# Four of eleven pairs of gate tiles computed by seven products of half blocks, with six gate tiles ahead of the first up unit

## What is computed

```python
D_FF = 2816
FFN_CONV_WIDTH = 3

def causal_dwconv(x, w):
    k_width = w.shape[0]
    s = x.shape[1]
    xp = jnp.pad(x, ((0, 0), (k_width - 1, 0), (0, 0)))
    return sum(xp[:, j:j + s] * w[j] for j in range(k_width))

        h = rmsnorm(x, ln2[l])
        gate = causal_dwconv(h @ w_gate[l], ffn_conv[l])
        x = x + (jax.nn.silu(gate) * (h @ w_up[l])) @ w_down[l]
    return rmsnorm(x, ln_f)
```

## Time and profile before

| | us |
|---|---|
| median of 3 runs | 2668.59 |
| lowest, highest | 2666.81, 2672.78 |
| the profiled execution | 2666.36 |
| its span, first to last instruction | 2664.5 |

### The profile page before, as it was taken

One profiled execution on the slowest core, in us unless ns is written; L12 is line 12 of the kernel. 1 busy time (PEld: TensorE's weight loads), 2 busy tenths in 40 slices (PEclk: granted clock), 3 DMA queues, 4 the chain that ended last, 5 costly groups with the idle time before them and its releaser, 6 DMA issues.

```text
span 2664.5 us, 36444 instructions
## 1 busy us (share of the span) xinstructions
PE 2474.7 (93%) x14220; PEld 1524.5 (57%) x14220; DVE 1385.3 (52%) x2603; ACT 1022.0 (38%) x1944; POOL 504.5 (19%) x342
## 2 busy tenths in 40 slices
PE   6998887899999999797969999999899998999998
PEld 4874566433333333675744434443677887788887
DVE  3596545335444445586442333333766654673745
ACT  5225552234444443626523222222453343442423
POOL 0222102001111011233100000000324311453533
PEclk9999999899999999899989999999999998999999
DMA  7215714689999998420039999999122011132221
GB/s 279 68 48 222 285 64 180 245 326 380 386 388 385 388 387 347 145 79 17 33 134 394 421 421 421 421 421 403 55 92 80 17 32 48 56 111 92 99 95 64
DMA packets 85514, 567.98 MB, mean 213 GB/s; under 512 B 11640, under 2 KB 12024, under 8 KB 20320
## 3 DMA queue, kind: packets, MB, share of 16 engines
q1 hardware_dynamic: 79944, 550.27, 52.4%
q0 software_dynamic: 3616, 11.80, 2.0%
q10 hardware_dynamic: 1784, 3.58, 0.4%
HBM read 550.92 MB, written 14.68 MB: 212 GB/s over the span
## 4 chain that ended last, share of the span: by engine, by line
PE 44%; DVE 3%; DMA 2%; ACT 1%; POOL 1%; issue 1%; DVEq 0%; ACTq 0%; POOLq 0%
PE PS L1193 11%; PE PS L1322 3%; PE PS L1323 3%; PE PS L1324 3%; PE PS L1310 2%; PE PS L1308 2%; PE PS L1309 2%; PE PS L1267 2%; PE PS L1298 2%; PE PS L932 1%; PE PS L1555 1%; PE PS L1557 1%; PE PS L1556 1%; DMA RF<-in_w_down_dram 1%; PE PS L1440 1%
## 5 line engine op out<-in xcount | busy, mean ns | idle before, releaser
L3004 POOL TENSOR_TENSOR WHL<-RING,WHL 128x1024 fp32r<-128x1024 f32 (+1 forms) x84 | 203.4, 2422 | 822.4 <-ACT WHL L1590 818.3
L1590 ACT ACTIVATE WHL<-RING 128x1024 fp32r<-128x1024 f32 (+1 forms) x158 | 149.8, 961 | 238.2 <-PE PS L1324 134.1
L1193 PE MATMUL PS<-RING,RF 128*64 128x512 f32 x816 | 187.2, 602 | 1.0 <-issue 0.7
L1193 PE MATMUL PS<-WIDE,RF 128*64 128x512 f32 x792 | 182.0, 596 | 0.0
L2169 DVE TENSOR_TENSOR WHL<-RING,WHL 128x1024 fp32r<-128x1024 f32 (+1 forms) x74 | 97.8, 1323 | 129.1 <-ACT WHL L1590 124.7
L1883 ACT ACTIVATE RF<-PS,MODS,MSC 128x128 f32<-128x128 f32 x192 | 73.2, 445 | 180.1 <-PE PS L1267 128.8
L1308 PE MATMUL PS<-RR,WHL 128*128 128x512 f32 x336 | 136.6, 406 | 3.7 <-DVE RR L2700 1.8
L1310 PE MATMUL PS<-RR,WHL 128*128 128x512 f32 x336 | 133.6, 398 | 0.0
L1309 PE MATMUL PS<-RR,WHL 128*128 128x512 f32 x336 | 132.6, 395 | 0.0
L1193 PE MATMUL PS<-RF 128*64 128x512 f32 x544 | 127.5, 596 | 0.4 <-DMA RF<-in_w_down_dram 0.4
L1193 PE MATMUL PS<-X,RF 128*64 128x512 f32 x528 | 123.0, 597 | 0.4 <-DMA X<-in_w_down_dram 0.4
(11 more groups left out here) (446 smaller groups left out, 5752.1 us busy)
## 6 DMA issues: line engine op xcount, KB each, us to landing
RING<-in_w_gate_dram SPq DMA_DIRECT2D x63, 1024.0 KB, 8.8
WIDE<-in_w_down_dram SPq DMA_DIRECT2D x52, 1024.0 KB, 11.9
RING<-in_w_up_dram SPq DMA_DIRECT2D x46, 1024.0 KB, 8.6
RING<-in_ada_w_dram SPq DMA_DIRECT2D x44, 1024.0 KB, 6.5
AR<-in_w_up_dram SPq DMA_DIRECT2D x37, 1024.0 KB, 10.4
X<-in_w_gate_dram SPq DMA_DIRECT2D x36, 1024.0 KB, 8.8
RF<-in_w_down_dram SPq DMA_DIRECT2D x31, 1024.0 KB, 13.8
RING<-in_w_in_dram SPq DMA_DIRECT2D x30, 1024.0 KB, 5.0
```

Source lines behind the costliest of these rows:

```text
L1193: ins = e.matmul(a[r:r + 64, :], xs[:, j, 0:64], w[:, i, :], start=begin and i < 2, stop=end and i > 1)
L1590: e.activation(h, unsplit(st), ACT.Copy).then_inc(act, A(("hi", st["i"])))
L3004: e.tensor_tensor(lo, unsplit(st), h.bitcast(F32), ALU.subtract).then_inc(pool, G(("lo", st["i"])))
```

## The change

Gate pairs 3, 5, 7 and 9 (`GATE7`) are also made by the seven products, with their own sums, splitting and additions. Their convolution can't read PSUM, so it reads `Q`: ACT makes the last tap (`tap`), DVE adds the other two (`conv7`, four instructions with both inputs in SBUF), then ACT does both `silu`.

PE's order is now: six gate tiles, up 0, gate pair 3, up 1, gates 8 and 9, up 2, gate pair 5, up 3, down; up 4, gates 12 and 13, up 5, gate pair 7, up 6, gates 16 and 17, up 7, down; up 8, gate pair 9, up 9, gates 20 and 21, up 10, down. The unit after a down product has its sums made during that product. Where a unit follows a unit, its sums stand at products 1 and 6 of the unit before it. The convolution of a direct gate tile stands one step of PE later than before. Of a unit's seven low parts POOL now makes those of products 7 and 3 (before: of 2 and 4), DVE the other five. On DVE and POOL the low parts listed beside a direct gate tile now stand one step of PE earlier; those listed beside a product of a unit stand as before, and the low parts of the first down weights, where they are listed beside a product, one step later.

```diff
+GATE7 = (3, 5, 7, 9)
...
-    ends = {t1 // 2 - 1: part for part, (t0, t1) in enumerate(FFN)}
-    order = [("gate", 0), ("gate", 1)]
-    for u in range(FFN[-1][1] // 2):
-        if u + 1 < FFN[-1][1] // 2:
-            order += [("gate", 2 * u + 2), ("gate", 2 * u + 3)]
-        order += [("product", u, p) for p in SEVEN]
-        if u in ends:
-            order += [("down", ends[u], 0), ("down", ends[u], 1)]
+    order, gates = [], 0
+    for part, (t0, t1) in enumerate(FFN):
+        for u in range(t0 // 2, t1 // 2):
+            while gates < min(u + 3 - part, FFN[-1][1] // 2) and not (part and u == t0 // 2):
+                if gates in GATE7:
+                    order += [("product", ("gate", gates), p) for p in SEVEN]
+                else:
+                    order += [("gate", 2 * gates), ("gate", 2 * gates + 1)]
+                gates += 1
+            order += [("product", ("up", u), p) for p in SEVEN]
+        order += [("down", part, 0), ("down", part, 1)]
...
+            if k[1] and following is not None:
+                plan += [("sum", following, i) for i in (1, 2, 3, 4)]
...
+        if waiting and (what == "gate" or k[1] == SEVEN[0]):
+            f = waiting.pop(0)
+            plan += [("conv", f), ("silu", f)]
...
+            (kind, u), p = k
+            if near and p in (1, 6) and order[n + 7 - SEVEN.index(p)][0] == "product":
+                plan += [("sum", following, i) for i in ((1, 2) if p == 1 else (3, 4))]
+            rest = [("gu", u), ("gh", u), ("gl", u)] if kind == "up" else [("tap", u), ("conv7", u), ("silu", 2 * u), ("silu", 2 * u + 1)]
+            plan += {1: [("E", k[0])], 6: [("U2", k[0]), ("C11", k[0])], 7: [("UB", k[0]), ("C22", k[0])],
+                     4: [("UC", k[0]), *rest]}.get(p, [])
...
-                          single=mode == "u", low=mode == "u" and m in (1, 6) or mode == "f" and cc % 256 == 128)
+                          single=mode == "u", low=mode == "u" and m in (4, 5) or mode == "f" and cc % 256 == 128)
...
-            late = n >= len(ahead) - (len(steps) - ffn) and loads[st["load"]]["name"] != "w_down2"
+            used = n - (len(ahead) - len(steps))
+            late = used >= ffn and steps[used]["single"]
...
+                elif what == "tap":
+                    u, = k
+                    e.wait_ge(dve, V["UC", ("gate", u)])
+                    if u > 2:
+                        e.wait_ge(dve, V["gl", u - 3])
+                    for h in range(2):
+                        w = V_FC + 44 + 2 * u + h
+                        e.activation(GS[u % 3][:, 512 * h:512 * h + 512], Q[:, 512 * h:512 * h + 512], ACT.Copy, scale=VEC[:, w:w + 1]
+                                     ).then_inc(act, A(("tap", 2 * u + h)))
...
+                elif what == "conv7":
+                    u, = k
+                    for j in range(2):
+                        for h in range(2):
+                            f, o, b = 2 * u + h, GS[u % 3][:, 512 * h:512 * h + 512], Q[:, 512 * h:512 * h + 512]
+                            w = V_FC + 22 * j + f
+                            if j == 0:
+                                e.wait_ge(act, A["tap", f])
+                            else:
+                                e.wait_ge(dve, V["shift", f])
+                            e.scalar_tensor_tensor(o[:, 2 - j:512], b[:, 0:510 + j], VEC[:, w:w + 1], o[:, 2 - j:512], ALU.mult, ALU.add
+                                                   ).then_inc(dve, V(("gate" if j else "shift", f)))
```

More of the change, by code:

```diff
@@ L113, in ffn_order @@
     return order
 def ffn_plan():
-    plan = []
-    for what, *k in ffn_order():
+    plan, order, waiting = [], ffn_order(), []
+    for n, (what, *k) in enumerate(order):
+        following = next((it[1] for it in order[n + 1:] if it[0] == "product" and it[2] == SEVEN[0]), None)
+        near = any(it[0] == "product" and it[2] == SEVEN[0] for it in order[n + 1:n + 8])
         if what == "down":
             plan += [(what, *k)]
+            if k[1] and following is not None:
+                plan += [("sum", following, i) for i in (1, 2, 3, 4)]
@@ L123, in ffn_plan @@
             continue
         plan += [("w",), (what, *k)]
+        if waiting and (what == "gate" or k[1] == SEVEN[0]):
+            f = waiting.pop(0)
+            plan += [("conv", f), ("silu", f)]
         if what == "gate":
             f, = k
-            if f > 1:
-                u = f // 2 - 1
-                plan += [("sum", u, 1 + f % 2 * 2), ("sum", u, 2 + f % 2 * 2)]
-            if f % 2 or f == 2:
-                plan += [("conv", f - 1), ("silu", f - 1)]
-            if 0 < f < 4:
-                plan += [("operand", {1: 5, 2: 6, 3: 7}[f])]
-        else:
-            u, p = k
-            last = FFN[-1][1] // 2 - 1
-            plan += {1: [("conv", 2 * u + 3), ("E", u), ("silu", 2 * u + 3)] if u < last else [("E", u)],
-                     2: [("operand", 4)] if u == 0 else [],
-                     6: [("U2", u), ("C11", u)], 7: [("UB", u), ("C22", u)], 4: [("UC", u), ("gu", u), ("gh", u), ("gl", u)]}.get(p, [])
-            if u == last - 1 and p in (6, 5):
-                plan += [("sum", last, i) for i in ((1, 2) if p == 6 else (3, 4))]
+            waiting.append(f)
+            if order[n + 2 - f % 2][0] == "product":
+                plan += [("sum", following, 1 + f % 2 * 2), ("sum", following, 2 + f % 2 * 2)]
+            if 0 < f < 5:
+                plan += [("operand", {1: 5, 2: 6, 3: 7, 4: 4}[f])]
+        else:
+            (kind, u), p = k
[4 more added lines that the diff above has]
+                     4: [("UC", k[0]), *rest]}.get(p, [])
@@ L232, in weight_steps @@
         elif what == "product" and more[0] == SEVEN[0]:
[L233 removed]
+            add("w_up2" if k[0] == "up" else "w_gate2", (), 0, 8, 256 * k[1], 256, "u")
             loads[-1]["unit"] = k
@@ L3173, in gpsimd @@
                     e.wait_ge(weights_in[ld["slot"]], 16 * ld["n"])
-                    if u:
-                        low_done(next(st for st in of_unit[u - 1]["steps"] if st["sum"] == i))
+                    if u in earlier:
+                        low_done(next(st for st in of_unit[earlier[u]]["steps"] if st["sum"] == i))
                     if i in (2, 4):
```

16 lines of the change are left out of this document (9 added, 7 removed).

## The result

The changed kernel takes 2680.48 us, median of 6 runs (2677.29 to 2682.44), the kernel before 2668.53 (6 runs, 2665.96 to 2672.78). The ratio is 1.0040 with a 95% interval of 1.0028 to 1.0052: slower by 12.0 us. That is 0.4% and clear of the spread of the runs. Forecast were 2680.0 and "slower", so the total came out as forecast. Several of its terms did not, and the experiments are about those.

The account below looks back on a forecast made before the run. PE was taken to bound the kernel. Products -4.5, gaps -8.6, start +3.2, chains +18.5 and clock +2.8 gave +11.4 us on the median of 2668.59: forecast 2680.0, range 2658 to 2690.

Parts of the forecast that it names:

- PE sets the time, products -4.5: Last stage: PE is the limit; four gate pairs at 10.08 instead of 11.20 us each save 4.5 us.
- The four gaps, -8.6: PE's waits and slow steps at gate 3, up 0, gate 4 and unit 10: 8.6 us saved if all went.
- The start, +3.2: Six gate tiles and up 0: 1.6 us stays at gate 3, 1.6 more for a late low part in up 0.
- the walk from gate 1 to product 7: DVE and ACT followed through gates 1 to 4: low part ready at 2332.3, PE wants it at 2330.7, 1.6 us lost.
- The chains, +18.5: Four runs of three successive units: DVE, taking turns with POOL, falls behind PE; losses 5.5, 5.1, 5.1 and 2.8 us.
- The wait behind `conv7`: Product 3 of the up unit after a gate unit: its low part comes 2.6 us late in the second chain.
- The signs named beforehand: Steps unchanged; two waits a chain, some 2 and 2.6 us; gate units' `UC` 3 us or more late; none at unit 10.
- The clock, +2.8: PE falling to 1.2 GHz behind long waits: two falls taken, between none and six, 1.4 us for one.
- The price of `conv7`: Each of its four DVE instructions was taken at 0.65 us, with 0.75 as upper bound.
- The sum: All terms together: +11.4 us, 2677.8 against the profiled execution, 2680.0 against the median.
- B: Rival, chance 0.22: DVE late only for `tap` and `conv7`, PE loses 2.6 us four times; +0.5 us, 2669.
- A: Rival, chance 0.20: the chains keep up, only waits at the start stay; -11.5 to -9.9 us, 2657 to 2659.

## Why the prediction was right, and where only in sum

- **PE sets the time, products -4.5.** Right. The steps are 0.233 and 0.120 as in the earlier trace rows, and the stage adds up to 0.1 us with them. The Trainium skill (TensorE: Matmul & The Clock Gate, section Back-to-back issue gap) would have four pairs cost 7 us more instead, by the prediction's estimate from its 81 and 131 ns, with 256 columns a third of the way up (the prediction says halfway). The traces disagree, with 120 and 233 ns, and the versions with and without gate units, both nearly free of waits, bear them out: 1.9 less.
- **The four gaps, -8.6.** Those at gate 4 and unit 10 went and that at gate 3 stayed, as foreseen. That at product 6 of up 0 should have gone, and 1.56 of it stayed. And 8.6 was the size in one execution; the second has 13.5 (9.7 in waits and 3.8 in slow steps). This base was taken for fixed.
- **The start, +3.2.** 5.4 in waits, with a clock fall 7.2. (There is also a slip in the prediction: 2307.96 + 3 x 5.6 + 4 x 1.44 is 2330.5 and not 2330.7, so its own numbers give 1.8 for 1.6.) The step that failed is the walk from gate 1 to product 7: it ends the convolution of gate 4 at 2329.8 and gives no loss at product 6. With the 3.8 by which the stage starts earlier in this trace added, that convolution ended at 2332.1 (2328.3), 2.3 later than walked, and the two high parts behind its `silu` began at once (2328.35 and 2328.89 in the rows above). That `silu` ahead of the high part is the cause is shown by the run that moved it, in which both waits go.
- **The chains, +18.5.** 13.6 measured. The wait behind `conv7` was sized well (2.6 against 2.75, 2.75, 2.73, 2.37), that behind `gh` not (2.1 against 0.77, 0.77, 1.41 and none). The timelines of DVE and ACT in the second chain, whose walk the prediction gives:

```profile
2385.31 0.68 DVE L3000 TENSOR_TENSOR CON<-PS,CON 128x512 f32<-128x512 f32 x1
2386.09 1.81 DVE L3017 TENSOR_TENSOR AR<-CON,AR 128x1024 f32<-128x1024 f32 x1
...
2397.59 0.68 DVE L3000 TENSOR_TENSOR CON<-PS,CON 128x512 f32<-128x512 f32 x1
2399.06 2.74 DVE L3011 SCALAR_TENSOR_TENSOR AR<-CON,VEC,AR 128x510 f32<-128x510 f32 x4 [0.79 <-ACT AR L2166]
```

```profile
2387.94 1.06 ACT L2175 ACTIVATE AS<-AR 128x1024 fp32r<-128x1024 f32 x1 [5.07 <-DVE AR L3017]
2388.91 0.61 ACT L1601 ACTIVATE WHL<-X 128x512 fp32r<-128x512 f32 x1
...
2398.30 1.34 ACT L2166 ACTIVATE AR<-CON,VEC 128x512 f32<-128x512 f32 x2 [4.45 <-DVE CON L3000]
2401.17 1.29 ACT L2158 ACTIVATE AR<-AR 128x512 f32<-128x512 f32 x2 [1.53 <-DVE AR L3011]
2402.37 0.61 ACT L1601 ACTIVATE WHL<-X 128x512 fp32r<-128x512 f32 x1
```

  From `UC` of up 2 (2385.31) to that of gate unit 5 (2397.59) DVE takes 12.3 us; the prediction says 12.2. But `UC` of up 2 starts 11.9 after PE's start on the unit (2373.4), not 13.9: the walk let the convolutions end at 4.9 and DVE's first low part at 8.1, and they ended at 3.7 and 5.9. So `UC` is 1.8 late and not 3.8, and the first wait is a third of what was forecast. That lateness is the step that failed. The second isn't shorter, because PE, held up less, wants product 3 earlier too. ACT idles 5.07 and 4.45 us with the high part next in its list, which is the mechanism as it was told; both the run with short sums and the one with `gh`, `tap`, `conv7` and `silu` at product 6 bear it out. The signs named beforehand came too: `UC` of the gate units 3.16, 3.16, 3.14 and 2.78 us behind PE (3 or more was said), and no wait at unit 10.
- **Not foreseen, +3.0.** The second step of the down product, 2.4. The prediction's section on the change has the low parts of the first down weights one step later, but gives it no price. DVE makes this one behind `UC`, `gu` and `gl`, and then waits out POOL's:

```profile
2411.84 4.54 DVE L2189 TENSOR_TENSOR WHL<-RING,WHL 128x1024 fp32r<-128x1024 f32 x2
```

```profile
2411.70 2.47 POOL L3037 TENSOR_TENSOR WHL<-RING,WHL 128x1024 fp32r<-128x1024 f32 x1 [4.49 <-ACT WHL L1601]
```

  Two wide low parts take 4.54 where 2.4 is their undisturbed length. The other 0.66 is gate 16 behind the third chain.
- **The clock, +2.8.** There were three falls, 4.5 us, where two were taken, and 1.2 of first slow steps behind the waits.
- **The price of `conv7`.** 0.65 was chosen, 0.75 was the bound. The source view sides with the bound, though four in a row pass in 2.74:

```profile
L3011 DVE SCALAR_TENSOR_TENSOR AR<-CON,VEC,AR x16: 741/744/751, 2352.4 to 2604.1; 128x510 f32<-128x510 f32 x8, 128x511 f32<-128x511 f32 x8
```

- **The sum.** Forecast +11.4, in the traces +14.7, in the medians +12.0. The term of the chains was 4.9 too large; the start (2.2), the down product and gate 16 (3.0) and the slow steps (2.9) were together 8.1 too small. The errors partly cancel, and that the median fits to 0.5 us is owed also to the short stage of the one execution of before on which the sum was built: with the second execution's 13.5 for 8.6 the same terms give +6.5, 2675.1. Sign, mechanism and the order of size are shown; that the totals meet is partly chance.
- **The rivals.** B (late only behind `conv7`) is nearer to the places than to the time: the waits behind `gh` are a fifth of the chains' loss. The version with every item moved comes to A's time and a little below (2654.7, A has 2657 to 2659 and keeps the gap at gate 3), so A was possible with these columns, not with this order.

## What to carry to other kernels

Where two engines take turns, walk each engine's list item by item and ask for every item that the bottleneck needs soon what stands ahead of it and could wait: here moving such items, without a single instruction removed, was worth 25 us of a stage of 381 (one execution of each), while the change of algorithm that they accompanied was worth 4.5 at best and 1.9 in fact. Compute less on the bottleneck only if the engines that feed it have room within each step, not on average. And profile the kernel before twice: a stage whose order hangs on which of two engines comes first by 0.4 us has more than one length.

## What the runs showed of the hardware

- Idle time of 2.2 to 2.6 us on PE brings the lower clock level in some cases and not in others. In the changed kernel 2.23, 2.59 and 2.20 did, 2.59, 2.57 and 2.21 did not; in two executions of the same kernel 2.45 did and 2.44 did not, and 1.85 did not and did. A fall costs 1.4 to 1.6 us.
- A DVE or POOL instruction with both inputs in SBUF that starts while the other engine's runs is held up by up to that one's rest. For wide low parts that is 2.81 and 3.12 us instead of 1.22, decided by 0.3 to 0.6 us of lead. The Trainium skill (SBUF — State Buffer, section SBUF: two separate sides) lets the loser wait for the whole of the other's instruction. By that rule an estimate from these rows is 2.35 - 0.61 + 1.22 = 2.96 and 2.35 - 0.31 + 1.22 = 3.26; the traces nearly agree, with 2.81 and 3.12.
- A slower clock can save time by changing which engine comes first: of two executions of the kernel before, the one that fell to 1.2 GHz at product 6 has the shorter stage, 366.1 against 371.1.
- The start of the stage, behind work that is the same in all kernels, lies between 2284.80 and 2296.90 us over 14 profiled executions. Spans of single executions can't be compared to better than that; stages can, but not to better than the 5 us of the kernel before.
